# The last two experts' rows added by an index matrix on TensorE instead of through memory

## The chip, the cores and the metric

One core of a Trainium2 chip runs the whole kernel. The metric is the device time of one execution in microseconds; lower is better.

## The reference

A decoder layer on 512 tokens of 1024 values, float32. Its first part (RWKV-7 time mixing beside block-sparse attention) is not touched here. The second is a mixture of 32 experts, of which each token uses two:

```python
xs = ht[tok]                                   # rows sorted by expert
hid = jax.nn.silu(lax.ragged_dot(xs, w1, sizes)) * lax.ragged_dot(xs, w3, sizes)
ys = lax.ragged_dot(hid, w2, sizes) * weights.reshape(-1)[order][:, None]
out = jax.ops.segment_sum(ys, tok, num_segments=T)
...
x = x + gate2 * out
```

w1 and w3 are 1024x512 and w2 is 512x1024 for each expert, 2 MB each, 201 MB in all.

## The kernel before, in words

P = 128 partitions, TT = 4 token tiles of 128 tokens, NEXP = 32 experts, SLOTS = 64 rows for each expert. An expert with more than 64 tokens gets further passes after the loop (n_over of them, a value read at run time; the trace shows none of them running). Five engines run lists of instructions written out by hand, each in its own order, and meet at semaphores.

- SP issues the weight loads: first the matrices of the first part (a loop over `items`, L344 to L378), then w1, w3 and w2 of each expert (`load_w13`, `load_w2`) into three sets of buffers (expert e uses set e % 3, and a load waits for the product of expert e - 3). All of them go through one queue in this order.
- POOL gathers an expert's 64 tokens (L757) from `h2_table` in memory into `picked`, two experts ahead, and writes its 64 finished rows of 4 KB (L762) into `y_rows`, a table in memory with 2 x 512 rows: row k * 512 + t is what the k-th choice of token t gives. A slot without a token has an index out of bounds, which the transfer skips.
- TensorE turns the gathered rows (L1678), forms the up products with w1 and w3 (`up`, L1685 and L1686), turns hid (L1691) and forms the down product with w2 (`down`, L1699). ACT takes the silu (L680) and copies what is turned (L675, L684).
- DVE multiplies silu and the second product to hid (L1229) and scales the down product's rows by the token's weight and by gate2 into `ys` (`weighted_rows`, L1222), two buffers of 64 partitions in `mod`.

The instructions of an expert are issued in the order: up, the next expert's turning, turning of hid, down. Matrix products are float32; one matmul of 512 columns appears in the trace as two instructions.

After the loop: POOL waits for all writes to `y_rows` and reads the number of further passes (L776), then tells SP (`y_stored`). SP reads `y_rows` back with eight transfers of 512 KB (L422), for each token tile t the two halves k = 0, 1, into `sum0` and `sum1`, which are the buffers W1_IN[2] and W3_IN[2] of the experts. For each tile DVE adds the halves (L1251) and adds the sum to x (L1252), 128x1024 each, and SP writes the tile to `out` (L425).

`rt` and `rt2` name parts of the constants and of `mod` that hold tables of the routing, free once the experts run. bank[i] are the eight PSUM banks of 128x512.

Of the kernel before, what the change touches and what calls it, by code (L numbers as in the profile page):

```python
# [79 lines left out]
def hybrid_layer(nc, A, out):  # L80
# [5 lines left out]
    with ctx:  # L86
        def sem(name):
            return ctx.enter_context(nc.semaphore(name))
# [64 lines left out]
        def group_part(k, at, n, heads=4):  # L153
# [28 lines left out]
        msc = [qkv[:, i, 512:1024] for i in range(4)]  # L182

        first.close()

# [39 lines left out]
        slot_hot = rt2[:, 512:1024].rearrange("p (j s) -> p j s", s=SLOTS)  # L225
        empty = rt[0:SLOTS, 468 + 8 * 8:468 + 8 * 8 + 2 * NEXP] if False else rt[0:SLOTS, 1024 + 768:1024 + 768 + 2 * NEXP]
        LE, CAND, PICK1, PICK2, PICKS, RANK = (rt2[:, 128 * i:128 * i + 128].rearrange("p (t n) -> p t n", n=NEXP) for i in range(6))
        ones = rt2[:, 896:1024]
        picked_to = LE
        sum0, sum1 = (f.rearrange("p (t n) -> p t n", t=TT) for f in (W1_IN[2], W3_IN[2]))  # L230
        h2_table = nc.dram_tensor("h2_table", [SEQ, D], f32).ap()
        y_rows = nc.dram_tensor("y_rows", [2 * SEQ, D], f32).ap()

        s_const, s_x, s_c, s_cols = sem("s_const"), sem("s_x"), sem("s_c"), sem("s_cols")
# [32 lines left out]
            "ov_mm", "ov_half", "ov_hid", "ov_ht", "ov_hte", "ov_y", "ov_ys", "ov_out"))  # L267
        s_sum, y_stored, s_final = [sem(f"s_sum{t}") for t in range(TT)], sem("y_stored"), sem("s_final")
        past = sem("past")
# [77 lines left out]
        def _(sp):  # L347
            sp.dma_start(x[:, :, :], A["x"].rearrange("(t p) d -> p t d", p=P)).then_inc(s_x, 16)
            sp.wait_ge(s_c, 16 * 12)
            for i, (src, _, _) in enumerate(items):  # L350
# [66 lines left out]

            sp.wait_ge(y_stored, 1)
            both = y_rows.rearrange("(k t p) d -> k p t d", k=2, p=P)
            for t in range(TT):  # L420
                for k in range(2):
                    sp.dma_start((sum0, sum1)[k][:, t, :], both[k][:, t, :]).then_inc(s_sum[t], 16)  # L422
            for t in range(TT):
                sp.wait_ge(s_final, t + 1)
                sp.dma_start(out[P * t:P * t + P, :], x[:, t, :]).then_inc(s_done, 16)  # L425
            sp.wait_ge(s_done, 16 * TT)

# [269 lines left out]
        def _(pool):  # L697
            made = [0]

            def seq(ins):  # L700
                made[0] += 1
                ins.then_inc(pool_chain, 1)
                pool.wait_ge(pool_chain, made[0])


            pool.wait_ge(prep_done, CT)
# [60 lines left out]
            gather(0)  # L767
            gather(1)
            for e in range(NEXP):
                if e + 2 < NEXP:  # L770
                    pool.wait_ge(xt_mm, e + 1)
                    gather(e + 2)
                scatter(e)
            for b in range(2):
                pool.wait_ge(y_out[b], 16 * NEXP // 2)
            n_over = pool.value_load(passes[0:1, 0:1], min_val=0, max_val=MAXOV)  # L776
            with pool.If(n_over > 0):
                with pool.Fori(0, n_over) as j:
# [3 lines left out]
                    pool.wait_ge(ov_now, 2 * j + 1)  # L782
# [3 lines left out]
                    pool.wait_ge(ov_ys, 2 * j + 2)  # L786
                    pool.sem_inc(past, 1)
                    pool.tensor_copy(now[0:SLOTS, 1:2], slot_rows[:, 1, bass.ds(j + NEXP, 1)]).then_inc(ov_now, 1)
                    pool.wait_ge(ov_now, 2 * j + 2)
                    pool.sem_inc(past, 1)  # L790
                    pool.indirect_dma_start(y_rows, IOA(now[0:SLOTS, 1:2].bitcast(u32), 0), ys[:, 0, :], None,
                                            bounds_check=2 * SEQ - 1, oob_is_err=False).then_inc(ov_out, 16)
                    pool.wait_ge(ov_out, 16 * j + 16)
                    pool.sem_inc(ov_ready, 1)
            pool.sem_inc(y_stored, 1)

        @block.vector
        def _(dve):
# [420 lines left out]

            def weighted_rows(e, b, done):  # L1220
                for n in range(2):
                    dve.scalar_tensor_tensor(ys[:, b, 512 * n:512 * n + 512], bank[5 + n][SLOTS * n:SLOTS * n + SLOTS, :], weight_of(e),  # L1222
                                             gate2[:, n, :], ALU.mult, ALU.mult).then_inc(done, 1)

            for e in range(NEXP):
                dve.wait_ge(silu_done, e + 1)
                if e:
                    dve.wait_ge(ht_mm, e)
                dve.tensor_tensor(hid[:, :], bank[3][SLOTS:P, :], silu_a[:, :], ALU.mult).then_inc(hid_v, 1)  # L1229
                if e == 0:  # L1230
                    dve.wait_ge(slots_mm, 2)
                    rows_of(bank[7][0:SLOTS, :], NEXP, MAXOV, gather_v)
                dve.wait_ge(w2_mm, e + 1)
# [5 lines left out]
            for b in range(2):  # L1239
                dve.wait_ge(y_out[b], 16 * NEXP // 2)  # L1240
            dve.sem_inc(ov_ready, 1)
            with dve.If(n_over > 0):
                with dve.Fori(0, n_over) as j:
# [3 lines left out]
                    weighted_rows(j + NEXP, 0, ov_ys)  # L1247

            for t in range(TT):
                dve.wait_ge(s_sum[t], 32)  # L1250
                seq(dve.tensor_tensor(sum0[:, t, :], sum0[:, t, :], sum1[:, t, :], ALU.add))  # L1251
                dve.tensor_tensor(x[:, t, :], x[:, t, :], sum0[:, t, :], ALU.add).then_inc(s_final, 1)  # L1252

        @block.tensor
        def _(pe):
# [475 lines left out]
            with pe.If(n_over > 0):  # L1731
                with pe.Fori(0, n_over) as j:
# [10 lines left out]
                    pe.wait_ge(ov_w2, 16 * j + 16)  # L1743
                    down(0).then_inc(ov_y, 1)


# [27 lines left out]
```

## Time and profile before

| | us |
|---|---|
| median of 3 runs | 1211.34 (1207.2 to 1211.41) |
| profiled execution | 1212.69 |
| its span | 1210.9 |
| TensorE busy | 1033.4 (85%) |
| DVE busy | 435.8 (36%) |
| POOL busy | 168.5 (14%) |
| mean granted clock of TensorE | 0.927 |
| memory read, written | 276.19 MB, 12.58 MB |

The span is cut into 40 slices of 30 us on the page. The transfers ran at 399 to 418 GB/s in the slices of the experts (from about 720 us on) and at 257 and 211 GB/s in the last two. In the chain of work that ended last, 23% of the span is loading of the experts' weights, 17% one line of products in the first part. A row of the chain or of an engine's timeline gives the start, the duration, the engine and line, and what was written from what; in brackets how long the engine had been idle and what released it. A clock of 1.00 is TensorE's full clock and 0.50 half of it.

### The profile page before, as it was taken

Reading aid. Unit: us, or ns where it says so; the run is one execution under the profiler, and the core shown is the slowest. Engines: PE = TensorE matmul, PEld = TensorE weight load, DVE = VectorE, ACT = ScalarE, POOL = GpSimd, SP = SyncE. Lnnn points to the kernel's source line nnn. Section 1 sums busy time; section 2 is a strip of 40 time slices with the busy share of each in tenths; the row PEclk is TensorE's granted clock in tenths of the full one; section 3 lists DMA queues with packets and bytes.
Section 4 is the critical chain, followed back from the end, with each engine's and each line's share of the span. In section 5 each row is a group of like instructions: output and inputs, shape, how many; then the busy total and the mean of one; then the engine's idle time right before and its main releaser. Section 6 shows DMA issues by size and latency. Waiting matters only on the chain.

```text
span 1210.9 us, 17785 instructions
## 1 busy us (share of the span) xinstructions
PE 1033.4 (85%) x7825; PEld 611.7 (51%) x7825; DVE 435.8 (36%) x718; ACT 278.1 (23%) x482; POOL 168.5 (14%) x194
## 2 busy tenths in 40 slices
PE   3799999989899789999998499998888887888781
PEld 2677644459897566666687233333333333333330
DVE  3765667673543753022356411111111111111113
ACT  5532043414142764011232011111111001111100
POOL 0000000036097440000000011111111111001100
PEclk9699999999797989999998599999999989999986
DMA  8847323000000212322085789999999999999965
GB/s 320 320 161 259 137 76 139 1 4 5 4 4 31 111 24 70 139 70 70 22 326 223 277 347 409 399 391 408 403 411 410 418 405 403 408 408 410 411 257 211
DMA packets 52755, 281.54 MB, mean 233 GB/s; under 512 B 7899, under 2 KB 9125, under 8 KB 40261
## 3 DMA queue, kind: packets, MB, share of 16 engines
q1 hardware_dynamic: 46480, 268.61, 56.4%
q0 software_dynamic: 5184, 8.47, 2.2%
q10 hardware_dynamic: 1014, 3.33, 0.7%
q8 instruction: 62, 1.02, 0.4%
q14 instruction: 15, 0.12, 0.0%
HBM read 276.19 MB, written 12.58 MB: 238 GB/s over the span
## 4 chain that ended last, share of the span: by engine, by line
PE 60%; DMA 27%; DVE 6%; ACT 3%; issue 2%; SPq 1%; ACTq 0%; POOLq 0%; DVEq 0%
DMA w_tok<-in_w 23%; PE banks L1292 17%; PE banks L1685 10%; PE banks L1321 7%; PE banks L1699 4%; PE banks L1596 4%; DMA tokm<-in_w_ada 2%; PE banks L1411 1%; PE banks L1413 1%; PE banks L1426 1%; DMA w_qkv<-y_rows 1%; DMA picked<-h_table,slot_rows 1%; PE banks L1553 1%; PE banks L1272 1%; PE banks L1447 1%
## 5 line engine op out<-in xcount | busy, mean ns | idle before, releaser
L1685 PE MATMUL banks<-w_ring,xT 128*64 128x512 f32 x336 | 156.0, 619 | 28.6 <-DMA w_ring<-in_w 16.6
L1229 DVE TENSOR_TENSOR hid<-banks,silu_a 64x512 f32<-64x512 f32 x32 | 22.2, 693 | 257.7 <-ACT silu_a L680 257.7
L680 ACT ACTIVATE silu_a<-banks 64x512 f32<-64x512 f32 x32 | 18.9, 591 | 409.3 <-PE banks L1686 409.3
L1685 PEld LDWEIGHTS banks<-w_ring,xT 128*64 128x64 f32 x336 | 46.8, 143 | 129.6 <-issue 129.6
L1222 DVE SCALAR_TENSOR_TENSOR mod<-banks,row_weight,mod 64x512 f32<-64x512 f32 x64 | 47.8, 747 | 173.2 <-PE banks L1699 172.2
L1699 PE MATMUL banks<-w_ring,hidT 128*64 128x512 f32 x352 | 93.7, 681 | 10.4 <-ACT hidT L684 10.4
L1292 PE MATMUL banks<-x_r,ring_r 128*128 128x512 f32 x240 | 98.0, 408 | 0.1
L1685 PE MATMUL banks<-w_ab,xT 128*64 128x512 f32 x176 | 83.2, 629 | 14.9 <-DMA w_tok<-in_w 14.2
L762 POOL DMA_INDIRECT y_rows<-mod,slot_rows x32 | 29.5, 921 | 432.3 <-DVE mod L1222 432.3
L1321 PE MATMUL banks<-ring,hT 128*128 128x512 f32 x192 | 85.0, 595 | 0.0
L1686 PE MATMUL banks<-w_tok,xT 128*64 128x512 f32 x176 | 83.4, 630 | 0.0
L1686 PE MATMUL banks<-w_ring,xT 128*64 128x512 f32 x176 | 81.1, 616 | 0.0
L1686 PE MATMUL banks<-w_qkv,xT 128*64 128x512 f32 x160 | 75.2, 625 | 0.0
L1685 PEld LDWEIGHTS banks<-w_ab,xT 128*64 128x64 f32 x176 | 24.8, 145 | 68.3 <-issue 67.5
L1321 PEld LDWEIGHTS banks<-ring,hT 128*128 128x128 f32 x192 | 35.8, 190 | 46.6 <-issue 46.1
L1699 PEld LDWEIGHTS banks<-w_ring,hidT 128*64 128x64 f32 x352 | 26.4, 154 | 61.4 <-issue 47.9
L1292 PEld LDWEIGHTS banks<-x_r,ring_r 128*128 128x128 f32 x240 | 45.6, 190 | 12.5 <-issue 1.9
L1292 PE MATMUL banks<-x_r,tokm_r 128*128 128x512 f32 x128 | 51.5, 402 | 0.0
L1678 PEld LDWEIGHTS banks<-consts,picked 64*128 64x128 f32 x256 | 30.6, 200 | 35.9 <-issue 24.3
L1292 PE MATMUL banks<-x_r,mid_r 128*128 128x512 f32 x112 | 45.6, 407 | 3.7 <-DVE hT_r L849 3.7
L564 ACT ACTIVATE ring<-banks 128x512 f32<-128x512 f32 (+1 forms) x64 | 33.1, 517 | 56.7 <-PE banks L1426 27.8
L1292 PE MATMUL banks<-hT_r,mid_r 128*128 128x512 f32 x112 | 44.7, 399 | 0.0
(339 smaller groups left out, 1983.3 us busy)
## 6 DMA issues: line engine op xcount, KB each, us to landing
w_ring<-in_w SPq DMA_DIRECT2D x54, 2048.0 KB, 36.0
w_tok<-in_w SPq DMA_DIRECT2D x21, 2048.0 KB, 38.3
w_ab<-in_w SPq DMA_DIRECT2D x11, 2048.0 KB, 35.1
w_qkv<-in_w SPq DMA_DIRECT2D x10, 2048.0 KB, 38.8
ring<-in_w_ada SPq DMA_DIRECT2D x8, 2048.0 KB, 8.2
ring<-in_w_in SPq DMA_DIRECT2D x7, 2048.0 KB, 8.0
tokm<-in_w_ada SPq DMA_DIRECT2D x4, 2048.0 KB, 14.9
tokm<-in_w_in SPq DMA_DIRECT2D x3, 2048.0 KB, 12.8
```

The costliest lines, as they stand in the source:

```text
L564: act.activation(dst.rearrange("p h n -> p (h n)"), src, ACT.Copy).then_inc(solve_a[k], 1)
L680: act.activation(silu_a[:, :], bank[2][0:SLOTS, :], ACT.Silu).then_inc(silu_done, 1)
L762: pool.indirect_dma_start(y_rows, IOA(slot_rows[:, 1, e:e + 1].bitcast(u32), 0), ys[:, e % 2, :], None, bounds_check=2 * SEQ - 1, oob_is_e ...
L1222: dve.scalar_tensor_tensor(ys[:, b, 512 * n:512 * n + 512], bank[5 + n][SLOTS * n:SLOTS * n + SLOTS, :], weight_of(e), gate2[:, n, :], ALU ...
L1229: dve.tensor_tensor(hid[:, :], bank[3][SLOTS:P, :], silu_a[:, :], ALU.mult).then_inc(hid_v, 1)
L1292: mm = pe.matmul(dst, a[i][:, k, col_a], b[l][:, k, col_b], start=(k == 0 and n == 0), stop=(k == KT - 1 and n == 2))
L1321: mm = pe.matmul(bank[6 + j % 2][:, :], hT[:, k, (j % TT) * P:(j % TT) * P + P], w[:, k, :], start=(k == 0), stop=(k == KT - 1))
L1596: pe.matmul(bank[j % 2][:, :], slot_view(at, CT)[:, k, P * ct:P * ct + P], (ahat, bhat)[b][:, k, :], start=(k == 0), stop=(k == CT - 1))
L1678: mm = pe.transpose(turned(b)[:, k, :], picked[0:SLOTS, b, k:D:KT], ident[0:SLOTS, 0:SLOTS])
L1685: pe.matmul(bank[2][0:SLOTS, :], xT[:, b, k, :], w1[:, k, :], start=(k == 0), stop=(k == KT - 1))
L1686: mm = pe.matmul(bank[3][SLOTS:P, :], xT[:, b, k, :], w3[:, k, :], start=(k == 0), stop=(k == KT - 1))
L1699: mm = pe.matmul(bank[5 + n][SLOTS * n:SLOTS * n + SLOTS, :], hidT[:, k, :], w2[:, k, 512 * n:512 * n + 512], start=(k == 0), stop=(k == 3))
```

## The change

- The rows of experts 30 and 31 are no longer written to `y_rows`. Expert 30's stay in buffer 0 of `ys` (partitions 0 to 63 of `mod[:, 2:4]`), expert 31's are written into partitions 64 to 127 of the same columns; together they are `last_rows`, 128x1024.
- DVE keeps the token number of each of these 128 slots (`last_token`, two copies ahead of expert 0) and in expert 2 forms `token_hot`, 128x512, which is 1 where a slot's token is the column's token.
- When expert 31's rows are weighted, TensorE forms `token_hot` transposed times `last_rows`: eight matmuls, one into each bank, and DVE adds each bank to its half tile of x. SP writes half tiles of 128x512 to `out`.
- As the tokens that experts 30 and 31 serve now have no row in `y_rows` for them, the table is cleared first: POOL clears a tile of 128x256, and SP writes it 32 times over (4 MB) ahead of item N_BEFORE_MERGE, before its wait for `gn_mm`. POOL waits for it ahead of its loop.
- SP reads `y_rows` back behind the weight loads of expert 31, once the rows of expert 29 are written and expert 29's up product is done. DVE adds tiles 0 and 1 (`sums`) between hid of expert 31 and the wait for its down product; POOL adds tiles 2 and 3 after its last write.
- The further passes add their rows with TensorE too; none runs here.

```diff
+        zeros = sb("zeros", [P, 256])
...
+        token_row, token_hot, token_hot_over = rt[:, 0:512], rt[:, 512:1024], rt[0:SLOTS, 1024:1536]
+        all_ones, last_token, over_token = rt[:, 1024:1536], rt[:, 1860:1861], rt[0:SLOTS, 1864:1864 + MAXOV]
+        last_rows = mod[:, 2:4, :].rearrange("p a n -> p (a n)")
+        NSCAT = NEXP - 2
...
                 if i == N_BEFORE_MERGE:
+                    sp.wait_ge(sums_g, 1)
+                    sp.dma_start(y_rows.rearrange("(p r) (a n) -> p (r a) n", p=P, n=256), zeros[:, :].unsqueeze(1).to_broadcast([P, 32, 256])).then_inc(y_zero, 16)
                     sp.wait_ge(gn_mm, 1)
...
+            for b in range(2):
+                sp.wait_ge(y_out[b], 16 * NSCAT // 2)
+            sp.wait_ge(up_mm, NSCAT)
+            both = y_rows.rearrange("(k t p) d -> k p t d", k=2, p=P)
+            for t in range(TT):
+                for k in range(2):
+                    sp.dma_start((sum0, sum1)[k][:, t, :], both[k][:, t, :]).then_inc(s_sum[t], 16)
+
             n_over = sp.value_load(passes[0:1, 0:1], min_val=0, max_val=MAXOV)
...
-            sp.wait_ge(y_stored, 1)
...
-                sp.wait_ge(s_final, t + 1)
-                sp.dma_start(out[P * t:P * t + P, :], x[:, t, :]).then_inc(s_done, 16)
+                for n in range(2):
+                    sp.wait_ge(s_final, 2 * t + n + 1)
+                    sp.dma_start(out[P * t:P * t + P, 512 * n:512 * n + 512], x[:, t, 512 * n:512 * n + 512]).then_inc(s_done, 16)
...
+            pool.memset(zeros[:, :], 0.0).then_inc(sums_g, 1)
...
+            pool.wait_ge(y_zero, 16)
             for e in range(NEXP):
                 if e + 2 < NEXP:
                     pool.wait_ge(xt_mm, e + 1)
                     gather(e + 2)
-                scatter(e)
-            for b in range(2):
-                pool.wait_ge(y_out[b], 16 * NEXP // 2)
+                if e < NSCAT:
+                    scatter(e)
+            for t in range(2, TT):
+                pool.wait_ge(s_sum[t], 32)
+                seq(pool.tensor_tensor(sum0[:, t, :], sum0[:, t, :], sum1[:, t, :], ALU.add))
+                pool.tensor_tensor(x[:, t, :], x[:, t, :], sum0[:, t, :], ALU.add).then_inc(sums_g, 1)
+
             n_over = pool.value_load(passes[0:1, 0:1], min_val=0, max_val=MAXOV)
...
-            pool.sem_inc(y_stored, 1)
...
             rows_of(bank[4][0:SLOTS, :], 0, NEXP, gather_v)
+            for i in range(2):
+                dve.tensor_copy(last_token[SLOTS * i:SLOTS * i + SLOTS, :], bank[4][0:SLOTS, NSCAT + i:NSCAT + i + 1])
...
+            def sums(t):
+                dve.wait_ge(s_sum[t], 32)
+                seq(dve.tensor_tensor(sum0[:, t, :], sum0[:, t, :], sum1[:, t, :], ALU.add))
+                seq(dve.tensor_tensor(x[:, t, :], x[:, t, :], sum0[:, t, :], ALU.add))
...
+                if e == 2:
+                    seq(dve.memset(all_ones, 1.0))
+                    seq(dve.tensor_tensor_scan(token_row, all_ones, all_ones, 0.0, ALU.mult, ALU.add))
+                    dve.tensor_scalar(token_hot, token_row, last_token, None, ALU.is_equal).then_inc(hot_v, 1)
+                if e == NEXP - 1:
+                    sums(0)
+                    sums(1)
                 dve.wait_ge(w2_mm, e + 1)
-                if e >= 2:
+                if 2 <= e < NEXP - 1:
                     dve.wait_ge(y_out[e % 2], 16 * (e // 2))
-                weighted_rows(e, e % 2, y_v)
+                weighted_rows(e, ys[:, e % 2, :] if e < NEXP - 1 else last_rows[SLOTS:P, :], y_v)
...
             for t in range(TT):
-                dve.wait_ge(s_sum[t], 32)
-                seq(dve.tensor_tensor(sum0[:, t, :], sum0[:, t, :], sum1[:, t, :], ALU.add))
-                dve.tensor_tensor(x[:, t, :], x[:, t, :], sum0[:, t, :], ALU.add).then_inc(s_final, 1)
+                if t == 2:
+                    dve.wait_ge(sums_g, 1 + TT - 2)
+                for n in range(2):
+                    xx = x[:, t, 512 * n:512 * n + 512]
+                    dve.wait_ge(last_mm, 2 * t + n + 1)
+                    dve.tensor_tensor(xx, xx, bank[2 * t + n][:, :], ALU.add).then_inc(s_final, 1)
...
+            pe.wait_ge(hot_v, 1)
+            pe.wait_ge(y_v, 2 * NEXP)
+            for i in range(2 * TT):
+                pe.matmul(bank[i][:, :], token_hot[:, P * (i // 2):P * (i // 2) + P], last_rows[:, 512 * (i % 2):512 * (i % 2) + 512],
+                          start=True, stop=True).then_inc(last_mm, 1)
```

## Rows read from the trace of the kernel before

**Rows 1.** the chain of waits of the tail: start, duration (us), what

```profile
1180.26 5.16 PE banks L1699 x16
1185.44 0.56 DVE mod L1222
...
1186.26 0.72 DVE mod L1222
...
1187.75 2.54 DMA y_rows<-mod,slot_rows
...
1190.38 0.50 POOLq L776
...
1195.10 10.19 DMA w_qkv<-y_rows
...
1206.57 1.23 DVE x L1252
```

**Rows 2.** the output issue at 1207.8: its time to landing

```profile
DMA to landing us min/median/max: 2.6/2.6/2.6
```

**Rows 3.** the DMA issues of SP, in order of time: start, duration

```profile
1137.10 0.33 SPq L401 DMA_DIRECT2D w_ring<-in_w  x1
...
1195.10 0.44 SPq L422 DMA_DIRECT2D w_qkv<-y_rows  x1
```

**Rows 4.** the issue at 1137.10, w2 of expert 31: its time to landing

```profile
DMA to landing us min/median/max: 38.1/38.1/38.1
```

**Rows 5.** POOL's write of expert 29's rows, issued 1156.9: time to landing

```profile
DMA to landing us min/median/max: 8.0/8.0/8.0
```

**Rows 6.** TensorE in order of time: a full-clock product

```profile
575.14 3.59 PE L1596 MATMUL banks<-bhat,ring 128*128 128x512 f32 x8
```

**Rows 7.** DVE in order of time, the tail

```profile
1178.35 0.69 DVE L1229 TENSOR_TENSOR hid<-banks,silu_a 64x512 f32<-64x512 f32 x1 [6.20 <-ACT silu_a L680]
...
1196.35 1.23 DVE L1251 TENSOR_TENSOR w_ring<-w_ring,w_qkv 128x1024 f32<-128x1024 f32 x1 [9.37 <-DMA w_qkv<-y_rows]
```

**Rows 8.** the chain of waits in experts 0 to 2

```profile
691.04 0.85 PE banks L1685
...
730.39 3.65 PE banks L1699 x16
```

**Rows 9.** stretches of 2 us: busy time by engine, TensorE's clock, DMA share, GB/s

```profile
1166.00:1168.00 2.00, 2.00 (x8) 0.65 (x6) 0.00 (x0) 0.00 (x0) 0.00 (x0) 0.55 0.66 274
1180.00:1182.00 2.00, 1.74 (x4) 0.53 (x6) 0.00 (x0) 0.21 (x1) 0.00 (x0) 0.50 0.01 4
1188.00:1190.00 2.00, 0.00 (x0) 0.00 (x0) 0.00 (x0) 0.00 (x0) 0.64 (x1) 1.00 0.23 49
```

**Rows 10.** POOL in order of time, two places

```profile
261.78 2.13 POOL L714 TENSOR_TENSOR x<-qkv 128x512 f32<-128x512 f32 x1
...
266.78 1.04 POOL L714 TENSOR_TENSOR x<-qkv 128x512 f32<-128x512 f32 x1
...
440.51 4.51 POOL L750 TENSOR_TENSOR hT_r<-hT,x_r 128x2048 fp32r<-128x2048 f32 x1 [11.77 <-ACT x_r L483]
```

**Rows 11.** DVE in order of time, the same places

```profile
260.72 2.29 DVE L929 TENSOR_TENSOR x<-consts,decay_end 128x2048 f32<-128x2048 f32 x1
...
442.10 2.94 DVE L1016 TENSOR_SCALAR zr<-zr 128x2 f32<-128x2 f32 x1
```

**Rows 12.** who SP waited for, 150 to 460: total, times, longest

```profile
SPq L362 <- PE banks L1508: 205.4, 1, 205.4
```

**Rows 13.** stretches as in rows 9, ahead of the merge

```profile
280.00:388.00 108.00, 99.18 (x3169) 97.62 (x3165) 42.95 (x103) 32.88 (x67) 62.42 (x76) 0.89 0.02 4
```

**Rows 14.** DVE in order of time, experts 0 to 2

```profile
700.34 0.69 DVE L1229 TENSOR_TENSOR hid<-banks,silu_a 64x512 f32<-64x512 f32 x1 [14.85 <-ACT silu_a L680]
...
734.10 1.53 DVE L1222 SCALAR_TENSOR_TENSOR mod<-banks,row_weight,mod 64x512 f32<-64x512 f32 x2 [4.92 <-PE banks L1699]
```

**Rows 15.** the groups by line and form: the scan of 512 columns

```profile
L886 DVE TENSOR_TENSOR_SCAN x<-consts,x 128x512 f32<-128x512 f32 x4 | 4.9, 1222 | 6.5 <-ACT x L528 6.5
```

More of the change, by code:

```diff
@@ L267, in hybrid_layer @@
             "ov_mm", "ov_half", "ov_hid", "ov_ht", "ov_hte", "ov_y", "ov_ys", "ov_out"))
-        s_sum, y_stored, s_final = [sem(f"s_sum{t}") for t in range(TT)], sem("y_stored"), sem("s_final")
+        s_sum, s_final = [sem(f"s_sum{t}") for t in range(TT)], sem("s_final")
+        y_zero, hot_v, last_mm, sums_g = sem("y_zero"), sem("hot_v"), sem("last_mm"), sem("sums_g")
         past = sem("past")
@@ L416, in _ @@
                         sp.dma_start(dst, src[bass.ds(e, 1)].rearrange("e p n -> (e p) n")).then_inc(landed, 16)
-            sp.wait_ge(y_stored, 1)
-            both = y_rows.rearrange("(k t p) d -> k p t d", k=2, p=P)
             for t in range(TT):
-                for k in range(2):
-                    sp.dma_start((sum0, sum1)[k][:, t, :], both[k][:, t, :]).then_inc(s_sum[t], 16)
-            for t in range(TT):
-                sp.wait_ge(s_final, t + 1)
-                sp.dma_start(out[P * t:P * t + P, :], x[:, t, :]).then_inc(s_done, 16)
-            sp.wait_ge(s_done, 16 * TT)
+                for n in range(2):
+                    sp.wait_ge(s_final, 2 * t + n + 1)
+                    sp.dma_start(out[P * t:P * t + P, 512 * n:512 * n + 512], x[:, t, 512 * n:512 * n + 512]).then_inc(s_done, 16)
+            sp.wait_ge(s_done, 16 * 2 * TT)
         def sum_bank(n):
@@ L1218, in _, with weighted_rows @@
             gate2 = mod[0:SLOTS, 6:8, :]
-            def weighted_rows(e, b, done):
+            def weighted_rows(e, dst, done):
                 for n in range(2):
-                    dve.scalar_tensor_tensor(ys[:, b, 512 * n:512 * n + 512], bank[5 + n][SLOTS * n:SLOTS * n + SLOTS, :], weight_of(e),
+                    dve.scalar_tensor_tensor(dst[:, 512 * n:512 * n + 512], bank[5 + n][SLOTS * n:SLOTS * n + SLOTS, :], weight_of(e),
                                              gate2[:, n, :], ALU.mult, ALU.mult).then_inc(done, 1)
+            def sums(t):
+                dve.wait_ge(s_sum[t], 32)
+                seq(dve.tensor_tensor(sum0[:, t, :], sum0[:, t, :], sum1[:, t, :], ALU.add))
+                seq(dve.tensor_tensor(x[:, t, :], x[:, t, :], sum0[:, t, :], ALU.add))
             for e in range(NEXP):
@@ L1232, in _ @@
                     rows_of(bank[7][0:SLOTS, :], NEXP, MAXOV, gather_v)
+                    dve.tensor_copy(over_token, bank[7][0:SLOTS, 0:MAXOV])
+                if e == 2:
[5 more added lines that the diff above has]
+                    sums(1)
                 dve.wait_ge(w2_mm, e + 1)
-                if e >= 2:
+                if 2 <= e < NEXP - 1:
                     dve.wait_ge(y_out[e % 2], 16 * (e // 2))
-                weighted_rows(e, e % 2, y_v)
+                weighted_rows(e, ys[:, e % 2, :] if e < NEXP - 1 else last_rows[SLOTS:P, :], y_v)
             n_over = dve.value_load(passes[0:1, 0:1], min_val=0, max_val=MAXOV)
-            for b in range(2):
-                dve.wait_ge(y_out[b], 16 * NEXP // 2)
-            dve.sem_inc(ov_ready, 1)
             with dve.If(n_over > 0):
+                for b in range(2):
+                    dve.wait_ge(y_out[b], 16 * NSCAT // 2)
+                dve.wait_ge(sums_g, 1 + TT - 2)
+                dve.sem_inc(ov_ready, 1)
                 with dve.Fori(0, n_over) as j:
@@ L1246, in _ @@
                     dve.wait_ge(ov_y, j + 1)
[L1247 to L1252 removed]
+                    dve.sem_inc(past, 1)
+                    dve.tensor_scalar(token_hot_over, token_row[0:SLOTS, :], over_token[:, bass.ds(j, 1)], None, ALU.is_equal)
+                    weighted_rows(j + NEXP, ys[:, 1, :], ov_ys)
+                    dve.wait_ge(ov_out, j + 1)
+                    dve.sem_inc(past, 1)
+                    for i in range(2 * TT):
+                        xx = x[:, i // 2, 512 * (i % 2):512 * (i % 2) + 512]
+                        ins = dve.tensor_tensor(xx, xx, bank[i][:, :], ALU.add)
+                    ins.then_inc(ov_ready, 1)
+            for t in range(TT):
+                if t == 2:
+                    dve.wait_ge(sums_g, 1 + TT - 2)
+                for n in range(2):
+                    xx = x[:, t, 512 * n:512 * n + 512]
+                    dve.wait_ge(last_mm, 2 * t + n + 1)
+                    dve.tensor_tensor(xx, xx, bank[2 * t + n][:, :], ALU.add).then_inc(s_final, 1)
         @block.tensor
@@ L1744, in _ @@
                     down(0).then_inc(ov_y, 1)
+                    pe.wait_ge(ov_ys, 2 * j + 2)
+                    pe.sem_inc(past, 1)
+                    for i in range(2 * TT):
+                        mm = pe.matmul(bank[i][:, :], token_hot_over[:, P * (i // 2):P * (i // 2) + P], ys[:, 1, 512 * (i % 2):512 * (i % 2) + 512],
+                                       start=True, stop=True)
+                    mm.then_inc(ov_out, 1)
+                    pe.wait_ge(ov_ready, j + 2)
+                    pe.sem_inc(past, 1)
+            pe.wait_ge(hot_v, 1)
+            pe.wait_ge(y_v, 2 * NEXP)
+            for i in range(2 * TT):
+                pe.matmul(bank[i][:, :], token_hot[:, P * (i // 2):P * (i // 2) + P], last_rows[:, 512 * (i % 2):512 * (i % 2) + 512],
+                          start=True, stop=True).then_inc(last_mm, 1)
 _INS = ["x", "c", "w_ada", "b_ada", "ln1_g", "ln2_g", "w_in", "mu_shift", "w0", "w_lora_up", "a0", "a_lora_up",
```

11 lines of the change are left out of this document (1 added, 10 removed).

## The prediction

> **What bounds the kernel now.** I read the end first, as the edit is nearly all there. The chain of waits, in order of time, shows the last link of real work: TensorE's down product of expert 31 ends at 1185.42 (1180.26 + 5.16), DVE weights the rows, POOL writes them to memory, SP reads all rows of y_rows back, DVE adds them [rows 1]. The reader is to see that from 1186.98 (the end of the two weightings, 1186.26 + 0.72) to 1207.80 (1206.57 + 1.23) TensorE does nothing: 20.8 us for a write, a read of 4 MB and two additions. From the last addition to the end of the span are 1210.9 - 1207.8 = 3.1 us, of which 2.6 are the last output transfer [rows 2]. The profiled execution took 1212.69 us with a span of 1210.9; the median of three is 1211.34, 1.35 below it. I sum on the profiled span and take 1.35 off at the end.
>
> Then the transfers. The last weight load, w2 of expert 31, is issued at 1137.10 and lands 38.1 us later, at 1175.2 [rows 3, 4]. The rows of expert 29 are issued by POOL at 1156.9 and land 8.0 us later, at 1164.9 [rows 5]. So between 1165 and 1192 the memory side has little to do, and all but two experts' rows are already there: that is the room which the change uses.
>
> **Part 1: the tail without the round trip.** Removed from the path: 1186.98 to 1207.80, 20.8 us. Put in its place: eight matmuls of 128x128 by 128x512, each followed by one DVE addition of a bank to x, the last one alone on the path. Four matmuls of that shape (eight instructions, two to a matmul) take 3.59 us at the full clock [rows 6], so eight take 7.2; the addition of a bank of 512 columns is like DVE's product for hid (0.69 [rows 7]) or a weighting (0.72 [rows 1]), I take 0.75 with its semaphore; 0.1 for the semaphore to TensorE. The tail behind the last addition stays 3.1; its transfer is half as large, which I leave at nothing. Clean end: 1186.98 + 0.1 + 7.2 + 0.75 + 3.1 = 1198.1, a gain of 12.8 us. The first seven additions and outputs lie under the matmuls (0.9 us apart against 0.75 for DVE and 0.44 for an issue by SP [rows 3]). Each engine now reads the pass count before its last work; from POOL's read (1190.38) to SP's next issue it cost 1.0 us [rows 1]. TensorE's read lies under the 1.5 us of weightings, SP's under the readback, DVE's under the first matmul. If TensorE's were not covered it would cost up to 1.0.
>
> **Part 2: TensorE's clock in the new work.** At the half clock the product records stand 0.85 us apart, as on the chain in expert 0 [rows 8], so the sixteen would take 13.6: bounds 7.2 and 13.6. TensorE is idle for about 1.6 us before them. In the last expert the granted clock was 0.50 in 1180 to 1182, right after the two short waits around hid [rows 9]; the down product took 5.16 there against 3.65 in expert 2 [rows 1, 8]. After that TensorE stood idle and 1188 to 1190 still shows 1.00 [rows 9]. I take one such slow stretch: 5.16 - 3.65 = 1.5 us. Kept for the range: 0 and 6.4.
>
> **Part 3: reading back early.** SP now waits for the writes of experts 28 and 29 (1164.9) and for the up product of expert 29 (long done, as its rows are being written), then issues eight reads of 512 KB, by 1169 at 0.44 each [rows 3]. They stand on SP's queue behind w2 of expert 31, whose last piece lands at 1175.2. I therefore count the reads from there. In the kernel before the reads took 10.2 us from the issue of the last to its landing, 1205.3, and the first addition could start at 1196.35 [rows 1, 7]: some 3 us for each token tile. So tile 0 is there at about 1178, tile 1 at 1181, tile 2 at 1183 (bounds 1179.5 and 1185), tile 3 at 1186. The loads of the experts aren't delayed, since they stand ahead.
>
> What is queued behind the new waits: on DVE, sums(0) and sums(1) stand between hid of expert 31 (ends 1179.04) and its weightings (from 1185.44), which TensorE waits for [rows 1, 7]. Four additions of 1.23 take 5.0 with their gaps [rows 7]: 1179.1 to 1184.2. That fits under the down product by 1.2 us. On POOL, tiles 2 and 3 take four additions of 128x1024; POOL's 128x2048 took 4.51 [rows 10], so 2.3 to 2.5 each, 9.6 in all: from 1183 to about 1193. DVE needs them when the fifth matmul is done, about 1194 with the two delays taken below. Zero, then, with that cover; each microsecond that POOL is later moves the end by nearly one.
>
> The cover has a hole. DVE and POOL exclude each other in this trace: POOL's L714 took 2.13 instead of 1.04 when DVE's 128x2048 product with two operands in SBUF ran from 260.72 to 263.01, and DVE's tiny L1016 took 2.94, until POOL's 128x2048 was over [rows 10, 11]. So an addition on POOL that starts among DVE's four pushes back those behind it, by up to 2.4 each. With tile 2 there at 1183, one POOL addition comes ahead of DVE's fourth: it ends at about 1186.5 instead of 1184.2, 1.1 later than the weightings could start. I take 1.0. If tile 2 landed by 1179 all four would alternate: 1179.0 + 4 x (1.23 + 2.4) = 1193.5, 8 us late at the worst, some 5 with one or two of them free. Lower bound 0.
>
> The Trainium skill (SBUF — State Buffer, "Who interferes with whom") says that a DVE instruction with two SBUF inputs and a GpSimd instruction that reads SBUF take one shared port in turn, for whole instructions; the trace agrees (2.13 against 1.04). By that page alone the additions of both engines can't overlap at all, while the weightings and the final additions, with one operand in PSUM, don't contend; the sum would be the same as mine, and the rule speaks against the split of the four tiles over two engines.
>
> **Part 4: the rest.** The zeroing: POOL clears 128x256 at the start, and SP writes 4 MB before its wait for gn_mm, in which it stood 205.4 us, until its next load; the DMA share in 280 to 388 is 0.02 [rows 12, 13]. A 4 MB transfer at the rate of the readback (12 us, up to four times that for pieces of 1 KB) is hidden there, and POOL's wait for it comes with the first experts, after 390. Nothing; if it were issued only after that wait it would stand before two weight loads and cost up to 12. On DVE two copies of a column come before expert 0, where DVE then idles 14.85, and in expert 2 a memset, a scan (1.22) and a comparison, 2.6 us in all, where it idles 4.92 before the weightings [rows 14, 15]. Nothing. Two writes of rows fewer: POOL is idle there. Nothing.
>
> **Sum.** 1198.1 + 1.5 (clock) + 1.0 (POOL against DVE) = 1200.6 of span, 10.3 below 1210.9; 1212.69 - 10.3 = 1202.4 for a profiled execution, 1201.0 against the median.
>
> **Rivals.**
> 1. Clean tail: neither a slow stretch nor a collision, or outputs that land sooner. For it: the clock stayed at 1.00 until 1190 though TensorE was idle since 1185.4 [rows 9]. 12.8 gained, 1198.5.
> 2. The additions collide throughout, because the reads land with the other queues' engines free and not after 1175.2. For it: the DMA share is down to 0.66 from 1166 on [rows 9], so most of the 16 engines are free by then. The weightings start some 5 late, then the slow stretch: 1198.5 + 5 + 1.5 = 1205, up to 1208.
> 3. TensorE at half clock in all eight: 1198.5 + 6.4 + 1.0 = 1206. Against it: the level came back within 4 us in the last expert.
> 4. Slower. DVE is in order, and sums(1) stands ahead of the weightings; each microsecond that tile 1 lands after 1182.9 moves the end by one. From 1182.9 + 10.3 = 1193 on the gain is gone. If the reads fared as the loads do (38.1 from issue to landing [rows 4]), tile 1 would land at 1167 + 38 = 1205; additions to 1207.5, weightings 1209, then 0.1 + 7.2 + 1.5 + 0.75 + 3.1: 1221.7 of span, 1222 against the median. Against it: nothing but the last weights is queued by then.
> 5. The reads don't start early (a wait of SP on something late), or the zeroing gets into the way: the round trip is replaced by a read that still ends last, about 1211.
>
> **How the numbers follow.** Chances: forecast 0.50, rival 1 0.20, rival 2 0.12, rival 3 0.06, rival 4 0.05, rival 5 0.07. A measurement can tell about 0.5% from no change, so 1205.3 is the border of faster and 1217.4 that of slower. Faster: 0.70 and about a third of rivals 2 and 3, 0.76. Slower: 0.06. Same: 0.18. The range takes in rivals 1 to 3: 1197.5 to 1207.5.
>
> **What would show it.** In the changed profile: no write of rows after about 1158; eight reads issued at about 1165 to 1169, the last landing by 1187; DVE's four additions between 1179 and 1187 and any of them or of POOL's longer than 1.23 or 2.4 where they meet; the weightings of expert 31 at 1185.4 to 1187; sixteen matmul records in 7 to 9 us behind them, at which clock the windows tell; the last output issued 0.8 after the last. The prediction is wrong if the first matmul of the tail starts after 1191, if the records take over 9 us, if TensorE's or SP's pass count costs more than 1, or if the stretch of the experts itself (to 1185.4) is no longer the same.

## The result and the profile after

The changed kernel takes 1196.26 us (median of 4 runs), the kernel before beside it 1209.73. The ratio is 0.989, with an interval of 0.987 to 0.991: faster, by 10.9 to 15.7 us. Forecast were 1201.0 and a range from 1197.5 to 1207.5, so it is 1.2 us better than the range allows. Two more sets of six runs gave 1196.32 and 1196.98, ratios 0.9902 (0.9868 to 0.9936) and 0.9911 (0.9886 to 0.9936), against 1209.56 and 1209.82 for the kernel before.

The profiled execution took 1195.67 with a span of 1193.8. Its chain of waits in the tail (start, duration, what), which answers to [rows 1]:

```profile
1150.21 7.81 DMA y_rows<-mod,slot_rows
...
1160.36 17.26 DMA w_qkv<-y_rows
...
1177.70 3.32 POOL w_ring L791
...
1181.09 2.36 POOL x L792
1183.44 2.31 POOL w_ring L791
...
1186.57 1.62 POOL x L792
...
1188.22 0.69 DVE x L1287
```

The long piece is a transfer of 17.3 us, from the issue of tile 2's second half to its landing at 1177.6. TensorE works beside it. What ends last is POOL, four additions one behind the other, then DVE's last four.

TensorE, DVE and POOL in order of time, and a stretch of 2 us inside the new matmuls (columns as in [rows 9]):

```profile
1173.95 0.69 PE L1726 MATMUL banks<-consts,hid 64*128 64x64 f32 x4 [1.41 <-DVE hid L1244]
1175.12 3.65 PE L1734 MATMUL banks<-w_ring,hidT 128*64 128x512 f32 x16 [0.47 <-ACT hidT L696]
1180.57 7.11 PE L1792 MATMUL banks<-mod,consts 128*128 128x512 f32 x16 [1.79 <-DVE mod L1232]
```

```profile
1182.00:1184.00 2.00, 2.00 (x6) 0.88 (x5) 1.66 (x3) 0.00 (x0) 2.00 (x2) 1.00 0.35 130
```

```profile
1173.20 0.69 DVE L1244 TENSOR_TENSOR hid<-banks,silu_a 64x512 f32<-64x512 f32 x1 [7.99 <-ACT silu_a L692]
1173.82 1.21 DVE L1237 TENSOR_TENSOR w_ring<-w_ring,w_qkv 128x1024 f32<-128x1024 f32 x1
...
1177.58 1.23 DVE L1238 TENSOR_TENSOR x<-x,w_ring 128x1024 f32<-128x1024 f32 x1
1178.89 1.53 DVE L1232 SCALAR_TENSOR_TENSOR mod<-banks,row_weight,mod 64x512 f32<-64x512 f32 x2
...
1184.27 0.69 DVE L1287 TENSOR_TENSOR x<-x,banks 128x512 f32<-128x512 f32 x1 [0.17 <-PE banks L1792]
1188.22 2.48 DVE L1287 TENSOR_TENSOR x<-x,banks 128x512 f32<-128x512 f32 x4 [3.25 <-POOL x L792]
```

```profile
1177.70 3.31 POOL L791 TENSOR_TENSOR w_ring<-w_ring,w_qkv 128x1024 f32<-128x1024 f32 x1 [26.57 <-DMA w_qkv<-y_rows]
...
1185.84 2.35 POOL L792 TENSOR_TENSOR x<-x,w_ring 128x1024 f32<-128x1024 f32 x1
```

DVE's four additions (1173.82 to 1178.81) end when the down product does (1178.77), so they don't hold the weightings back. The eight matmuls follow 1.8 us behind the down product and take 7.11 at a granted clock of 1.00. DVE adds four banks as they come, then stands 3.25 us for POOL. POOL's first addition took 3.31 against 2.35 for the others: it was released at 1177.70, 0.1 after DVE's fourth had begun, and seems to have stood until that was over.

### The profile page after: what moved, and what is told of

It reads as the page before. It is cut to its first block, busy times and chain, and to the rows that moved or that the text cites. A ratio compares the mean times of both kernels' runs of the same rounds, so it can differ in the third digit from the quotient of the medians.

```text
span 1193.8 us, 17834 instructions
## 1 busy us (share of the span) xinstructions
PE 1034.4 (87%) x7841; PEld 610.2 (51%) x7841; DVE 439.0 (37%) x728; ACT 277.8 (23%) x482; POOL 177.7 (15%) x197
## 4 chain that ended last, share of the span: by engine, by line
PE 59%; DMA 28%; DVE 6%; ACT 3%; issue 2%; POOL 1%; SPq 1%; ACTq 0%; POOLq 0%; DVEq 0%
PE banks L1327 17%; DMA w_ring<-in_w 13%; DMA w_qkv<-in_w 10%; PE banks L1720 10%; PE banks L1356 7%; PE banks L1631 4%; PE banks L1734 3%; DMA tokm<-in_w_ada 2%; DMA w_qkv<-y_rows 1%; PE banks L1446 1%; PE banks L1448 1%; PE banks L1461 1%; PE banks L1588 1%; DMA picked<-h_table,slot_rows 1%; PE banks L1307 1%
## 5 line engine op out<-in xcount | busy, mean ns | idle before, releaser
L1720 PE MATMUL banks<-w_ring,xT 128*64 128x512 f32 x336 | 155.4, 617 | 25.2 <-DMA w_ring<-in_w 18.8
L1721 PE MATMUL banks<-w_ring,xT 128*64 128x512 f32 x176 | 85.2, 641 | 0.0
L1721 PE MATMUL banks<-w_qkv,xT 128*64 128x512 f32 x160 | 70.5, 594 | 0.0
L1327 PEld LDWEIGHTS banks<-x_r,ring_r 128*128 128x128 f32 x240 | 45.6, 190 | 12.6 <-issue 1.9
## 6 DMA issues: line engine op xcount, KB each, us to landing
tokm<-in_w_in SPq DMA_DIRECT2D x3, 2048.0 KB, 12.9
```

Of the source, the lines that this page charges most:

```text
L1327: mm = pe.matmul(dst, a[i][:, k, col_a], b[l][:, k, col_b], start=(k == 0 and n == 0), stop=(k == KT - 1 and n == 2))
L1720: pe.matmul(bank[2][0:SLOTS, :], xT[:, b, k, :], w1[:, k, :], start=(k == 0), stop=(k == KT - 1))
L1721: mm = pe.matmul(bank[3][SLOTS:P, :], xT[:, b, k, :], w3[:, k, :], start=(k == 0), stop=(k == KT - 1))
```

## What the two profiles differ by

The spans differ by 17.1 us, more than the medians (13.5). The start of expert 31's hid product, which the change hardly touches, is at 1178.35 before [rows 7] and 1173.20 after. I therefore count the *tail* from there to the end of the span: 32.6 before, 20.6 after, 12.0 less. The other 5.1 us lie ahead of it. Some of them were there before the experts began: SP's first load behind its wait for gn_mm is issued at 389.56 before and 385.36 after. Either the change speeds that stretch, or executions differ by as much.

## Experiments

**Same kernel again, and the zeroing alone.** Three kernels: the kernel before and the changed one, each run again without an edit, and the kernel before with this edit:

```diff
+        zeros = sb("zeros", [P, 256])
         first.close()
...
                 if i == N_BEFORE_MERGE:
+                    sp.wait_ge(zero_g, 1)
+                    sp.dma_start(y_rows.rearrange("(p r) (a n) -> p (r a) n", p=P, n=256), zeros[:, :].unsqueeze(1).to_broadcast([P, 32, 256])).then_inc(y_zero, 16)
...
+            pool.memset(zeros[:, :], 0.0).then_inc(zero_g, 1)
...
+            pool.wait_ge(y_zero, 16)
             for e in range(NEXP):
```

> The kernel before, unchanged. The first pair of profiles differs by 17.1 us of span, of which 5.15 lie ahead of expert 31's hid product (1178.35 against 1173.20), where the change does next to nothing. Theory A: that part is how far two executions differ (slow stretches of TensorE's clock fall elsewhere); then this profile puts that product anywhere from 1173 to 1179, and the time is 1207 to 1212. Theory B: the change speeds the stretch ahead of the tail; then this profile puts it at 1178 again, within 1 us.

> The changed kernel, unchanged. Theory A: hid of expert 31 starts anywhere from 1173 to 1179, the time 1195 to 1201. Theory B: at 1173 again, within 1 us, the time 1196. By both the tail from there to the end of the span is about 20.6 us, 19 to 24 according to the clock in the down product and in the eight new matmuls.

> The kernel before with the zeroing alone: POOL clears the tile, SP writes 4 MB ahead of its wait for gn_mm, POOL waits for it ahead of its loop. Theory A: no difference beyond 0.3%, about 1210, hid of expert 31 between 1173 and 1179. Theory B, in the form that the zeroing or where it stands moves what follows it: some 4 us faster, 1206, and the product at 1174.

| kernel | median, us | ratio (interval) | hid of expert 31 | tail |
|---|---|---|---|---|
| before, first profile | | | 1178.35 | 32.6 |
| before_again | 1210.45 | 1.0017 (0.999 to 1.0044) | 1172.76 | 31.4 |
| zero_only | 1209.65 | 1.0003 (0.9977 to 1.0029) | 1174.11 | 33.2 |
| after, first profile | 1196.26 | 0.989 (0.987 to 0.991) | 1173.20 | 20.6 |
| after_again | 1196.32 | 0.9902 (0.9868 to 0.9936) | 1173.66 | 20.5 |

The unchanged kernel before puts that product at 1172.76, 5.6 us sooner than its own first profile. Over the thirteen profiles of this case it starts anywhere from 1171.5 to 1179.0, with and without the change (1172.8 to 1178.4 for the kernel before, 1172.9 to 1173.7 for the changed one, 1171.5 to 1179.0 for its variants). So theory A holds: 5.1 us is no more than two executions of one kernel differ by, and the kernel before alone ran from 1202.41 to 1214.48 in 29 runs. The zeroing costs nothing that its interval of 0.3% either way can show: its 4 MB were issued at 211.8 in the changed kernel and landed 12.6 us later. One of the twelve executions of zero_only took 3471.2 us. The ratio leaves it out, and nothing on record explains it; no other run of this case did that. That the slow stretches of TensorE's clock make these differences was only seen in part. In the stretch 385 to 695 the mean granted clock was 0.93 in four profiles with the product at 1172.9 to 1174.1, and 0.91 in five with it at 1176.6 to 1178.8; but one with 0.91 has it at 1171.5, and of three with 0.92 two have it at 1172.8 and 1173.7 and one at 1179.0.

**The reading late.** TensorE's part stays, the reads are issued when expert 31's rows are weighted:

```diff
             sp.wait_ge(up_mm, NSCAT)
+            sp.wait_ge(y_v, 2 * NEXP)
...
-                if e == NEXP - 1:
-                    sums(0)
-                    sums(1)
...
+            sums(0)
+            sums(1)
             n_over = dve.value_load(passes[0:1, 0:1], min_val=0, max_val=MAXOV)
```

> The changed kernel with its reads of y_rows issued only when expert 31's rows are weighted, and DVE's two sums behind those weightings. By my sum the early reading is worth most of the gain: reads from 1.5 us after the down product, the last landing 14 us after the first issue as in the kernel before, then POOL's last tile (4.7) and four additions: about 1204. If it is the write of the last rows that costs and the reading is cheap, 1198 to 1200.

1209.71, ratio 1.0 (0.9977 to 1.0023): the whole gain is gone, and the time is 5.7 us longer than I expected. POOL in order of time, then DVE:

```profile
1196.59 2.35 POOL L792 TENSOR_TENSOR w_ring<-w_ring,w_qkv 128x1024 f32<-128x1024 f32 x1 [40.39 <-DMA w_qkv<-y_rows]
...
1203.73 2.34 POOL L793 TENSOR_TENSOR x<-x,w_ring 128x1024 f32<-128x1024 f32 x1
```

```profile
1197.70 2.48 DVE L1288 TENSOR_TENSOR x<-x,banks 128x512 f32<-128x512 f32 x4 [1.17 <-issue]
1206.11 2.48 DVE L1288 TENSOR_TENSOR x<-x,banks 128x512 f32<-128x512 f32 x4 [5.93 <-POOL x L793]
```

Tile 2 lands at 1196.6, and all four additions of POOL follow on the path, 9.5 us, not the last two that I had counted: tile 3 lands while POOL is at tile 2. The next run takes POOL out of it. Its reads are as late; `sums(0)` and `sums(1)` no longer stand behind the weightings, as each tile's sums now come right ahead of its banks:

```diff
-                seq(pool.tensor_tensor(sum0[:, t, :], sum0[:, t, :], sum1[:, t, :], ALU.add))
-                pool.tensor_tensor(x[:, t, :], x[:, t, :], sum0[:, t, :], ALU.add).then_inc(sums_g, 1)
+                pool.sem_inc(sums_g, 1)
...
             for t in range(TT):
-                if t == 2:
-                    dve.wait_ge(sums_g, 1 + TT - 2)
+                sums(t)
                 for n in range(2):
```

> The changed kernel with its reads issued late as in late_read, but with all four tiles added by DVE, behind the weightings, as in the kernel before; POOL adds nothing. This is TensorE's part of the change without the early reading. In late_read POOL's four additions ran one after the other from the landing of tile 2 and ended 9.5 us later, and the whole came out at 1209.7, no gain. If that was POOL's doing: the last tile lands 14 us after the first read's issue, 2.5 for its sums and 1.3 for its two banks, end 3.1 later: tail 30, 1205. If it is the reading itself that holds the time: 1209 again.

1206.91, ratio 0.9981 (0.9964 to 0.9998), tail 31.3.

```profile
1192.65 1.23 DVE L1237 TENSOR_TENSOR w_ring<-w_ring,w_qkv 128x1024 f32<-128x1024 f32 x1 [4.97 <-DMA w_qkv<-y_rows]
...
1206.31 1.29 DVE L1283 TENSOR_TENSOR x<-x,banks 128x512 f32<-128x512 f32 x2
```

Here DVE's own row of sixteen additions is the path, from 1192.65 to 1207.60 without a gap, and not the landing of the last tile that I had counted; the median is 1.9 us above the expected 1205. TensorE's part without the early reading is thus worth 0.2%, at most 4.4 us, and with POOL doing half the sums late_read shows no gain from it. By the medians of one chip, 1206.91 against 1196.98 for the changed kernel, the remaining 9.9 us come with the early reading, together with POOL's half of the sums, which this run does not have. The two parts can't be had in the other order: only because the last rows no longer pass through memory can the reading begin early.

**POOL's additions.** Left out altogether, the edit being the first half of the last diff (tiles 2 and 3 of the output lack their sums):

> The changed kernel without POOL's four additions: tiles 2 and 3 of the output lack what the rows in memory hold for them. The tail is counted from the start of expert 31's hid product to the end of the span; it took 20.6 and 20.5 us in two profiles of the changed kernel. Theory P (POOL's additions end last): TensorE's eight matmuls end 14.5 after hid, then 0.7 and 3.1: tail 18.3, so 2.3 us less, 1194. Theory C (they are covered, as the prediction had it): tail 20.6, no difference.

1196.62, ratio 0.9897 (0.9869 to 0.9924): no less than the changed kernel's 1196.3 to 1197.0. Its tail is 19.2. The expectation of 18.3 was drawn from a profile with a down product of 3.65 us; in this one it took 5.20. Below, a "slow" down product is one of 5.13 to 5.35 us, a "fast" one takes 3.65. So I set it beside a third profile of the changed kernel (six profiles had shown the 7.1 by then, not seven):

> The changed kernel once more, beside the two others on the same chip. Expected 1196 to 1197; hid of expert 31 anywhere between 1171 and 1179; the eight new matmuls in 7.1 us at the full clock, as in the seven profiles so far in which they start within 2 us of the down product's end.

```profile
1174.83 5.35 PE L1734 MATMUL banks<-w_ring,hidT 128*64 128x512 f32 x16 [0.47 <-ACT hidT L696]
1181.98 7.11 PE L1792 MATMUL banks<-mod,consts 128*128 128x512 f32 x16 [1.80 <-DVE mod L1232]
```

```profile
1180.30 1.53 DVE L1232 SCALAR_TENSOR_TENSOR mod<-banks,row_weight,mod 64x512 f32<-64x512 f32 x2 [1.78 <-PE banks L1734]
...
1187.92 2.48 DVE L1287 TENSOR_TENSOR x<-x,banks 128x512 f32<-128x512 f32 x4 [1.55 <-POOL x L792]
```

The down product takes 5.35, TensorE's last matmul ends at 1189.1, 1.2 later than POOL's last addition (1187.9). DVE still has four banks to add at 0.62 each and ends at 1190.4, where after the last matmul alone it would end at 1189.8. Tail 20.6; without POOL 19.2, of which 0.7 is that only 2.4 us follow the last addition instead of 3.1. DVE's additions, and with them the outputs, come 0.86 apart there and in a burst here; that this makes the 0.7 is not shown, and fine_wait below speaks against it. POOL's cost, counted to the last addition, is therefore 0.6 us with a slow down product, which eleven of the thirteen profiles have (5.13 to 5.35), and 2.3 with a fast one (the first profile: POOL ends 0.5 after TensorE, and DVE at 1190.70 instead of 1188.4). By the profiles theory P is right that POOL holds up the end, but with a slow down product that is worth a quarter of the 2.3 us expected: TensorE then ends after POOL, and only DVE's four banks that waited for POOL are late. The medians of six runs can't tell P from C.

Waiting tile by tile:

```diff
-                if t == 2:
-                    dve.wait_ge(sums_g, 1 + TT - 2)
+                if t >= 2:
+                    dve.wait_ge(sums_g, t)
```

> The changed kernel, where DVE waits for POOL tile by tile: banks 4 and 5 only for tile 2, banks 6 and 7 for tile 3. Theory P: POOL is done with tile 2 at 10.2 after hid and with tile 3 at 15.0, so only two additions are left behind it: tail 19.4, 1.2 us less. Theory C: no difference.

1196.1, ratio 0.988 (0.9847 to 0.9914), tail 20.6 with a down product of 5.35. DVE ended at 1194.13, 0.7 behind TensorE's last matmul at 1193.41, so POOL was off the path and the last addition 0.6 sooner after hid than in after_third (16.9 against 17.5), but 3.7 us followed it instead of 3.1, 1.6 of them after the last output had landed. The expected 1.2 us less did not come: no difference shown.

On top of that wait, the last sum is given to DVE:

```diff
             for t in range(2, TT):
                 pool.wait_ge(s_sum[t], 32)
-                seq(pool.tensor_tensor(sum0[:, t, :], sum0[:, t, :], sum1[:, t, :], ALU.add))
+                if t == 2:
+                    seq(pool.tensor_tensor(sum0[:, t, :], sum0[:, t, :], sum1[:, t, :], ALU.add))
+                else:
+                    pool.wait_ge(hot_v, 2)
...
+            dve.wait_ge(s_sum[3], 32)
+            dve.tensor_tensor(sum0[:, 3, :], sum0[:, 3, :], sum1[:, 3, :], ALU.add).then_inc(hot_v, 1)
```

> As the last, and DVE also forms the sum of the two halves of tile 3, behind expert 31's weightings, where it idles 1.3 us before the first matmul is done; POOL has three additions instead of four. Theory P: POOL ends 2.4 earlier, less what the two exclude each other for (DVE's may wait for POOL's second to begin, up to 1.2); TensorE then ends last: tail 18.3 to 18.8, 2 us less than the changed kernel, 1194. Theory C: no difference or slower by up to 1.2, as DVE's own row gets longer.

1195.35, ratio 0.9884 (0.9856 to 0.9912), tail 19.4 with a down product of 5.35: 1.2 less than after_third, TensorE last; expected were 18.3 to 18.8 and 1194.

```profile
1180.48 2.37 DVE L1265 TENSOR_TENSOR w_ring<-w_ring,w_qkv 128x1024 f32<-128x1024 f32 x1
```

DVE's new sum took 2.37 instead of 1.23: POOL's second addition ran until 1181.77, and 1.1 more is one addition of DVE's. Of the 1.2 us, 0.6 lie ahead of the last addition and 0.6 behind it (2.5 against 3.1).

**Letting the two engines meet.** Tiles 2 and 3 are read first:

```diff
-            for t in range(TT):
+            for t in (2, 3, 0, 1):
                 for k in range(2):
                     sp.dma_start((sum0, sum1)[k][:, t, :], both[k][:, t, :]).then_inc(s_sum[t], 16)
```

> The changed kernel with the reads of tiles 2 and 3 issued ahead of tiles 0 and 1, so that POOL's additions and DVE's meet. Theory X (DVE and POOL take turns for whole instructions): POOL works from about the hid product on, DVE's four additions take turns with it and end about 13 us after hid instead of 5.5, the weightings follow, tail 26, 5.5 us more, 1202. Theory N (no exclusion between these additions): DVE ends when its own tile 1 is there, 9 after hid; tail 21.9, 1.3 us more.

1205.52, ratio 0.9959 (0.9939 to 0.9979), tail 27.4: theory X, with a tail 1.4 us and a median 3.5 us above what it expected. DVE, POOL and TensorE in order of time:

```profile
1181.85 3.26 DVE L1237 TENSOR_TENSOR w_ring<-w_ring,w_qkv 128x1024 f32<-128x1024 f32 x1 [3.76 <-DMA w_qkv<-y_rows]
1185.15 3.24 DVE L1238 TENSOR_TENSOR x<-x,w_ring 128x1024 f32<-128x1024 f32 x1
1188.43 1.23 DVE L1237 TENSOR_TENSOR w_ring<-w_ring,w_qkv 128x1024 f32<-128x1024 f32 x1
```

```profile
1176.95 2.35 POOL L791 TENSOR_TENSOR w_ring<-w_ring,w_qkv 128x1024 f32<-128x1024 f32 x1 [20.15 <-DMA w_qkv<-y_rows]
...
1181.69 2.35 POOL L791 TENSOR_TENSOR w_ring<-w_ring,w_qkv 128x1024 f32<-128x1024 f32 x1
1184.11 3.20 POOL L792 TENSOR_TENSOR x<-x,w_ring 128x1024 f32<-128x1024 f32 x1
```

```profile
1192.63 8.96 PE L1792 MATMUL banks<-mod,consts 128*128 128x512 f32 x16 [7.99 <-DVE mod L1232]
```

DVE's first addition is released at 1181.85, 0.16 after POOL's third has begun, and ends 1.1 after that one's end (1184.04); POOL's fourth (3.20) waits for it in turn, and DVE's second (3.24) for that. Alone again, DVE takes 1.23. Besides, tile 0 was there only 4.4 us after hid began. And TensorE, idle for 8 us, needs 8.96 for the matmuls instead of 7.11: its granted clock was 1.00 in 1184 to 1188, when it was already idle, and 0.50 in 1190 to 1196, back to 1.00 from 1198.

**An earlier start for TensorE.** On top of shared_sums, TensorE starts with two matmuls on the first half of the columns once the first weighting is done:

```diff
+        LAST_ORDER = [(0, 0), (1, 0), (0, 1), (1, 1), (2, 0), (2, 1), (3, 0), (3, 1)]
...
-            pe.wait_ge(y_v, 2 * NEXP)
-            for i in range(2 * TT):
+            pe.wait_ge(y_v, 2 * NEXP - 1)
+            for j, i in enumerate(2 * t + n for t, n in LAST_ORDER):
+                if j == 2:
+                    pe.wait_ge(y_v, 2 * NEXP)
```

(DVE and SP go through the banks in the same order.)

> shared_sums (three additions on POOL, waits tile by tile), and TensorE starts on the first half of the columns when expert 31's first weighting is done, 0.76 before the second: its order is the first halves of tiles 0 and 1, then their second halves, then tiles 2 and 3. If TensorE ends last, tail 18.6 with a slow down product (shared_sums: 19.4, changed kernel: 20.5), about 1194.5. If POOL or DVE end last, as shared_sums, 1195.3.

1194.41, ratio 0.9886 (0.986 to 0.9911), against 1196.98 for the changed kernel on the same chip; its runs went from 1193.33 to 1196.99, those of the changed kernel there from 1195.37 to 1199.40. It is faster than the kernel before beyond doubt; against the changed kernel the two ratios' intervals overlap (0.986 to 0.9911 and 0.9886 to 0.9936), so that gain is likely and not shown.

```profile
1180.60 1.53 DVE L1235 SCALAR_TENSOR_TENSOR mod<-banks,row_weight,mod 64x512 f32<-64x512 f32 x2 [1.78 <-PE banks L1739]
1182.16 2.38 DVE L1265 TENSOR_TENSOR w_ring<-w_ring,w_qkv 128x1024 f32<-128x1024 f32 x1
1184.58 4.87 DVE L1292 TENSOR_TENSOR x<-x,banks 128x512 f32<-128x512 f32 x8
```

```profile
1181.49 7.10 PE L1799 MATMUL banks<-mod,consts 128*128 128x512 f32 x16 [1.01 <-DVE mod L1235]
```

TensorE starts 0.6 us before the second weighting is done, 1.0 behind the down product. The last addition ends 16.2 us after hid, 16.9 in shared_sums and 17.5 in after_third. But DVE's sum holds back the first bank until 1184.58, the eight additions and their outputs follow in one burst, and 3.1 us come behind them instead of 2.5: the tail is 19.4 as in shared_sums. Against the changed kernel the profile shows 1.2 us in the tail, where the medians differ by 2.6; the rest I put down to the spread of the runs.

## Why the prediction was wrong

The direction and the main mechanism were right: the round trip left the path, and eight matmuls took its place. The step that failed is the adding of two delays to the clean end, 1.5 us of slow clock and 1.0 of POOL against DVE. Neither came, and a term that I had put at nothing, POOL's end, took 0.6 to 2.3 us in their place. Besides, the time of the kernel before from which I subtracted was 1.8 us too high. In the terms of the sum:

- *Clean end, 12.8 us.* Right. The matmuls took 7.11 (7.2 said), the end after the last addition 3.1 (3.1 said), the last output landed in 2.3. From the start of the weightings to the end of the span it was 25.5 before and 13.2 in after_again, both with a slow down product: 12.3 less, to which POOL's 0.6 is to be added for the clean figure, 12.9.
- *The clock, 1.5 us.* Wrong. The step put one slow stretch into the new matmuls because the down product before had one. In all nine profiles in which they start within 2 us of the down product's end they took 7.10 or 7.11. The slow stretch stays in the down product (granted clock 0.50 in 1176 to 1178 of after_third), where the kernel before has it as well (5.16 in its first profile, 5.14 in zero_only, though 3.65 in before_again), so it largely cancels. Charging it once more was counting it twice. pool_first shows that the new matmuls can be slow, after 8 us without work.
- *DVE against POOL, 1.0 us.* The exclusion is real, the place was wrong. Tile 2 was there 4.4 to 4.5 us after hid in each profile of the changed kernel (predicted: 4.65, 1183 against 1178.35), but DVE's fourth addition had begun 0.1 before. So POOL waited and DVE did not. The prediction's own numbers say the same: three additions of 1.26 behind 1179.1 put the fourth at 1182.9, ahead of tile 2 at 1183, and the 1.0 should have been 0. With a margin of 0.1 us that was close: pool_first shows what the other order costs.
- *POOL's end, 0 us.* Wrong. "Zero, then, with that cover" took the fifth matmul at 1194, with both delays above. Without them it is done 2.5 us sooner, at 1191.6 by the same sum, ahead of POOL's 1193. POOL's time itself was well predicted: its last addition ended 15.0 us after hid began (predicted: 14.65). So DVE waits for POOL: 2.3 us at the end in the first profile, 0.6 with a slow down product. That each microsecond of POOL's moves the end by nearly one was tested by no run that delays POOL alone.
- *Reading early, zeroing, DVE's work in expert 2, pass counts.* Nothing to be seen, as said. w2 of expert 31 landed 3.0 us ahead of hid in the changed kernel and 3.15 before, so the loads weren't delayed; the last read landed 9.9 us after those weights (predicted: 1186 - 1175.2 = 10.8). The reads did not wait their turn behind the weights, though, as I had counted them: the first halves of tiles 0 and 1 (issued 1158.08 and 1158.93, 7.9 and 9.7 us to landing) were there at 1166.0 and 1168.6, ahead of w2 at 1170.2. The second halves came later, 2.5 us apart. That the tiles still came within 1 us of the predicted times is in part luck.
- *The rest.* The terms as they should have been are 12.8 less 0.6 to 2.3: 10.5 to 12.2, where I had 10.3. The medians of the three sets say 12.8 to 13.5, the first with an interval from 10.9 to 15.7. And the three runs of before on which I set my number, 1211.34, were on the slow side: 1209.6 in 29 runs. These 1.8 us alone carry the result out of the range; a gain of 13.5 from 1211.34 would have been 1197.8. The round trip varies too: from the start of the weightings to the end of the span the kernel before took 25.5 us in the profile that I summed on, 25.8 in before_again and 26.1 in zero_only, which has the same tail. By the tails with a slow down product, 32.6 and 33.2 against 20.5 and 20.6, the gain is 12.0 to 12.7; with a fast one it is 31.4 less 20.6, 10.8. Whether the last microsecond up to the medians' 13.5 lies elsewhere or in their spread stays open.
- *A sign of being wrong that misled.* The prediction was to be wrong if the stretch of the experts itself (to 1185.4) changed. The down product ended at 1178.8 instead, but the kernel before, run again, ended it at 1178.3: the sign can't tell a change from the spread of executions.

Of the rivals, the first (clean tail, 0.20) came nearest, 1198.5. The fourth was built on DVE waiting for a tile ahead of its weightings; in pool_first it does, and that together with the turns of the two engines takes more than half of the gain without making the kernel slower. What I missed is that single executions of the kernel before differ by 12 us in 29 runs, against a range of 10 for the forecast.

## What to carry to other kernels

A read that can't begin before the last product should be split so that all but the last piece is read while the engines still work: here that brought 9.9 of 13 us, while the new arithmetic, which makes it possible, brought 0.2% by itself. Before giving half of a sum to POOL, line up both engines' instructions in time: POOL takes 2.35 where DVE takes 1.23, and where both add tiles in SBUF they take turns, so that one addition each lasts 3.6 us and two on DVE 2.5. No run gives all four tiles to DVE with the early reads, so whether the split is better than none stays open. A slow stretch of the clock that the trace of before already contains is not to be charged to the change a second time, and a median of three runs is not to be taken for the kernel's time when single runs differ by 1%.

## What the runs showed of the hardware that I had not expected

- The eight matmuls ran at the full clock in nine profiles, 1.0 to 1.8 us after a product that had itself been partly slow in eight of them; after 8 us of idle they took 8.96, with a granted clock of 0.50 at their start.
- DVE and POOL took turns, one addition each, when both had a row of them in pool_first: 3.26 and 3.24 against 1.23 on DVE, 3.20 against 2.35 on POOL; in the changed kernel, where they meet once, POOL's took 3.31. The Trainium skill (SBUF — State Buffer, "Who interferes with whom") states that a DVE instruction with two SBUF inputs contends with a GpSimd instruction that reads SBUF; the trace agrees, 3.26 against 1.23.
- Two reads of 512 KB, issued 24 and 25 us after a 2 MB load on the same engine's queue, landed 4.2 and 1.6 us before it.
- The kernel before ran from 1200.83 to 1216.01 in all its runs here, the changed kernel from 1193.33 to 1199.40 in sixteen.
